# Expert 0's 0/1 columns built ahead of tile 3's normalisation, and its gather in another order

## What is computed

```python
x = layer_norm(DN_ALPHA * x + merged @ w_out[l], ln1_g[l], ln1_b[l])
# grouped_moe
probs = jax.nn.softmax(xt @ w_router + b_router, axis=-1)   # group by its two best, then top 2 inside it
gates = ...                                                  # (rows, 16), two of them not zero
for e in range(N_EXPERTS):
    h = jax.nn.silu(xt @ w_gate[e]) * (xt @ w_up[e])
    out = out + gates[:, e:e + 1] * (h @ w_down[e])
x = layer_norm(DN_ALPHA * x + moe, ln2_g[l], ln2_b[l])
```

## Time and profile before

| | |
|---|---|
| median of 3 runs | 833.96 us (833.56 to 834.3) |
| span of the profiled execution | 831.3 us |
| TensorE busy | 821.0 us, 99% of the span |
| VectorE busy | 579.2 us, 70% |
| ScalarE busy | 450.6 us, 54% |
| chain that ended last | 97% TensorE, 2% VectorE |
| mean granted TensorE clock | 0.995 |

### The profile page before, as it was taken

One profiled execution on the slowest core, in us unless ns is written; L12 is line 12 of the kernel. 1 busy time (PEld: TensorE's weight loads), 2 busy tenths in 40 slices (PEclk: granted clock), 3 DMA queues, 4 the chain that ended last, 5 costly groups with the idle time before them and its releaser, 6 DMA issues.

```text
span 831.3 us, 11149 instructions
## 1 busy us (share of the span) xinstructions
PE 821.0 (99%) x3833; PEld 682.0 (82%) x3833; DVE 579.2 (70%) x672; ACT 450.6 (54%) x456; POOL 73.3 (9%) x73
## 2 busy tenths in 40 slices
PE   9999999999999999999999999999999999999995
PEld 8888888888888888888888888888888888888873
DVE  5877434434557885432455588898899899899978
ACT  4655424433466663333233333578887887878640
POOL 1000000100000000000000000622211111100121
PEclk9999999999999999999999999999999999999999
DMA  6333324553233323234432926699999999999582
GB/s 209 93 109 90 101 84 148 200 177 101 76 101 101 101 88 114 85 94 139 151 90 77 352 102 253 203 320 418 388 393 397 395 394 390 400 377 384 227 317 106
DMA packets 112338, 173.45 MB, mean 209 GB/s; under 512 B 7402, under 2 KB 90003, under 8 KB 100534
## 3 DMA queue, kind: packets, MB, share of 16 engines
q1 hardware_dynamic: 106486, 159.80, 54.7%
q0 software_dynamic: 5824, 13.30, 4.4%
HBM read 163.49 MB, written 16.30 MB: 216 GB/s over the span
## 4 chain that ended last, share of the span: by engine, by line
PE 97%; DVE 2%; ACT 0%; issue 0%; DVEq 0%; POOL 0%; POOLq 0%
PE psA L689 8%; PE psA L691 8%; PE psA L690 8%; PE psA L876 7%; PE psA L878 7%; PE psA L877 7%; PE psB L691 6%; PE psB L690 6%; PE psB L689 6%; PE psB L903 3%; PE psB L902 3%; PE psB L901 3%; PE psD L691 2%; PE psC L691 2%; PE psD L690 2%; PE psC L689 2%
## 5 line engine op out<-in xcount | busy, mean ns | idle before, releaser
L1588 DVE TENSOR_TENSOR elo<-est,ehi 128x2048 fp32r<-128x2048 f32 x94 | 211.1, 2287 | 26.0 <-ACT ehi L1206 25.8
L1206 ACT ACTIVATE ehi<-est 128x2048 fp32r<-128x2048 f32 x94 | 177.6, 1917 | 41.5 <-DMA est<-in_w_exp_down_dram 24.9
L1378 DVE TENSOR_TENSOR wlo<-wst,whi 128x1024 fp32r<-128x1024 f32 (+1 forms) x76 | 95.0, 1251 | 86.5 <-ACT whi L1037 85.3
L1037 ACT ACTIVATE whi<-wst 128x1024 fp32r<-128x1024 f32 (+1 forms) x76 | 81.9, 1078 | 77.2 <-PE psB L691 30.7
L876 PE MATMUL psA<-ehi,xe_hi 128*128 128x512 f32 x256 | 101.4, 396 | 0.0
L878 PE MATMUL psA<-ehi,xe_lo 128*128 128x512 f32 x256 | 100.0, 390 | 0.0
L877 PE MATMUL psA<-elo,xe_hi 128*128 128x512 f32 x256 | 99.7, 390 | 0.0
L689 PE MATMUL psB<-xT_hi,whi 128*128 128x512 f32 x208 | 81.1, 390 | 0.0
L691 PE MATMUL psB<-xT_hi,wlo 128*128 128x512 f32 x208 | 81.0, 389 | 0.0
L690 PE MATMUL psB<-xT_lo,whi 128*128 128x512 f32 x208 | 81.0, 389 | 0.0
L878 PEld LDWEIGHTS psA<-ehi,xe_lo 128*128 128x128 f32 x256 | 48.1, 188 | 10.2
(11 more groups left out here) (371 smaller groups left out, 1536.3 us busy)
## 6 DMA issues: line engine op xcount, KB each, us to landing
est<-in_w_exp_gate_dram SPq DMA_DIRECT2D x32, 1024.0 KB, 12.3
est<-in_w_exp_up_dram SPq DMA_DIRECT2D x32, 1024.0 KB, 11.4
est<-in_w_exp_down_dram SPq DMA_DIRECT2D x32, 1024.0 KB, 12.5
wst<-in_w_in_dram SPq DMA_DIRECT2D x60, 512.0 KB, 3.9
wst<-in_w_branch_r_dram SPq DMA_DIRECT2D x8, 640.0 KB, 4.3
ys<-zero POOLq DMA_DIRECT2D x8, 512.0 KB, 2.9
wst<-in_w_branch_a_dram SPq DMA_DIRECT2D x8, 512.0 KB, 3.6
o_st<-in_w_out_dram SPq DMA_DIRECT2D x8, 512.0 KB, 4.4
```

The lines of the kernel that those rows point to most:

```text
L1037: A(whi[p][:, 0:K, :], wst[p][:, 0:K, :], ACT.Copy).then_inc(w_hi, 1)
L1206: A(ehi[s][:], est[s][:], ACT.Copy).then_inc(gu_hi if s < 4 else d_hi, 1)
L1378: V.tensor_tensor(wlo[p][:, 0:K, :], wst[p][:, 0:K, :], whi[p][:, 0:K, :], ALU.subtract).then_inc(w_lo, 1)
L1588: V.tensor_tensor(elo[s][:], est[s][:], ehi[s][:], ALU.subtract).then_inc(gu_lo if s < 4 else d_lo, 1)
```

## The change

Four things are changed. TensorE's two groups of unread products go from 14 to 12 and from 6 to 2. VectorE makes only expert 0's key first, and adds its positions and compares at once, so that `first_by` stands ahead of both halves of tile 3's normalisation; the keys of experts 1 to 3 are made between the halves, their additions behind. TensorE's gather for expert 0 takes tiles 0 to 2 for four blocks, waits for tile 3's half, takes tile 3 for these four, and then the same for the other four; `picks(1)` stands ahead of the last four products instead of between the halves. And VectorE's `rows_half(0)` stands right behind `listed(1)`, ahead of the row arithmetic.

```diff
             pe.wait_ge(gu_hi, 1)
-            warm(14, psC[1][:, 1, :])
+            warm(12, psC[1][:, 1, :])
...
-            warm(6, psB[0])
+            def first_rows(k, t):
+                return pe.matmul(psC[0][:, k // 4, (k % 4) * P:(k % 4 + 1) * P], x1[:, t, k * P:(k + 1) * P],
+                                 first_by[:, t, :], start=(t == 0 and k % 4 == 0),
+                                 stop=(t == TT - 1 and k % 4 == 3))
+
+            warm(2, psB[0])
             pe.wait_ge(x1_done, TT - 1)
-            pe.wait_ge(x1_half, 1)
-            for k in range(KD):
-                if k == 4:
-                    pe.wait_ge(x1_done, TT)
-                for t in range(TT):
-                    if k == 0:
-                        pe.wait_ge(first_done, t + 1)
-                    mm = pe.matmul(psC[0][:, k // 4, (k % 4) * P:(k % 4 + 1) * P], x1[:, t, k * P:(k + 1) * P],
-                                   first_by[:, t, :], start=(t == 0), stop=(t == TT - 1))
-                if k == 3:
-                    mm.then_inc(x0_t, 1)
+            for h, (done, count) in enumerate(((x1_half, 1), (x1_done, TT))):
+                for k in range(4 * h, 4 * h + 4):
+                    for t in range(TT - 1):
+                        if k == 0:
+                            pe.wait_ge(first_done, t + 1)
+                        first_rows(k, t)
+                pe.wait_ge(done, count)
+                if h == 0:
+                    pe.wait_ge(first_done, TT)
+                else:
                     pe.wait_ge(by_done, 1)
                     picks(1)
-            mm.then_inc(xe_t, 1)
+                for k in range(4 * h, 4 * h + 4):
+                    mm = first_rows(k, TT - 1)
+                mm.then_inc((x0_t, xe_t)[h], 1)
             gate_up(0, first=True, parts=range(1))
             pe.wait_ge(by_done, 2)
             picks(2)
...
             dve.wait_ge(sel_done, 1)
-            for e in range(4):
-                ins = V.tensor_scalar(keys[:, e, :], sel[:, :, e], -1000.0, 1000.0, ALU.mult, ALU.add)
-            chain.link(ins)
-
-            spread_half(TT - 1, 0, x1_half)
+            chain.link(V.tensor_scalar(keys[:, 0, :], sel[:, :, 0], -1000.0, 1000.0, ALU.mult, ALU.add))
             dve.wait_ge(pos_done, 1)
...
-            for e in range(4):
-                V.tensor_tensor(keys[:, e, :], keys[:, e, :], at_pos[:, :, e], ALU.add).then_inc(key_done, 1)
+            V.tensor_tensor(keys[:, 0, :], keys[:, 0, :], at_pos[:, :, 0], ALU.add).then_inc(key_done, 1)
             dve.wait_ge(key_done, 1)
             for t in range(TT):
                 V.tensor_scalar(first_by[:, t, :], slots[:], keys[:, 0, t:t + 1], None, ALU.is_equal
                                 ).then_inc(first_done, 1)
+            spread_half(TT - 1, 0, x1_half)
+            for e in range(1, 4):
+                ins = V.tensor_scalar(keys[:, e, :], sel[:, :, e], -1000.0, 1000.0, ALU.mult, ALU.add)
+            chain.link(ins)
             spread_half(TT - 1, 1, x1_done)
+            for e in range(1, 4):
+                V.tensor_tensor(keys[:, e, :], keys[:, e, :], at_pos[:, :, e], ALU.add).then_inc(key_done, 1)
             listed(1)
+            rows_half(0)
```

More of the change, by code:

```diff
@@ L1749, in picked, with rows_half @@
                                 None, ALU.add).then_inc(pick_done, 1)
-            for e in range(4):
-                V.tensor_tensor(keys[:, e, :], keys[:, e, :], at_pos[:, :, e], ALU.add).then_inc(key_done, 1)
+            def rows_half(q):
+                dve.wait_ge((x0_h, xe_h)[q], 1)
+                V.tensor_tensor(xe_lo[:, 4 * q:4 * q + 4], psC[0][:, q, :].rearrange("p (k c) -> p k c", c=P),
+                                xe_hi[:, 4 * q:4 * q + 4], ALU.subtract).then_inc((x0_l, xe_l)[q], 1)
+            V.tensor_tensor(keys[:, 0, :], keys[:, 0, :], at_pos[:, :, 0], ALU.add).then_inc(key_done, 1)
             dve.wait_ge(key_done, 1)
@@ L1778, in _ @@
             chain.link(V.tensor_scalar(dest[:], rowsum[:], -1.0, None, ALU.add))
[L1780 to L1785, removed]
             paid = [r16[6], r16[7]]
```

## The result

| | median | lowest to highest | executions |
|---|---|---|---|
| kernel before | 833.45 us | 833.09 to 834.30 | 8 |
| changed kernel | 835.34 us | 833.81 to 836.70 | 8 |

The ratio is 1.002, with a 95% interval of 1.001 to 1.0029: slower by 1.9 us at the median. That is small, but the whole interval lies above 1. The changed kernel scatters over 2.9 us, the kernel before over 1.2. The profiled execution of the changed kernel is one of its shorter ones, 834.16 us with a span of 832.5.

A forecast was written before the change was run, and what follows sets the result against it. TensorE's stream was taken to bound the kernel. Its gather gains 1.33 us but then waits for VectorE's list for expert 2, 0.70 later: 833.96 + 0.70 = 834.7 us, range 833.1 to 836.4.

The forecast's parts named there:

- What bounds: TensorE's stream: it waits for no DMA engine, expert turns take 17.75 us, so seam shifts reach the end one for one.
- The gather 1.33 earlier: TensorE's gather for expert 0 starts at 511.97 instead of 513.30, as its first column tile comes 1.33 us earlier.
- List 2 0.70 later: VectorE's 0/1 columns for expert 2, awaited by TensorE's picks for expert 2, end at 524.15 instead of 523.45.
- the hole before the first addition: VectorE idle for about 0.46 us, after the first key, waiting for TensorE's positions.
- The rule of free waits: Skill's rule that semaphores between chained VectorE instructions cost nothing extra; by it loss 0.45, time 834.4; forecast kept 0.70.
- The gain does not arrive: The gather's 1.33 us is lost waiting for expert 2's list; the rival that it arrives, 832.6 us, had chance 0.08.
- Nothing breaks in the queues: Queues that follow stay covered: expert 1's rows land at 524.8, wanted at 527.2, covered by 2.4 us.
- The clock: Rival: TensorE's clock halves for 3.41 us behind the wait at expert 2's picks, costing 1.7 us, 836.4; chance 0.12.
- the prediction's own sign: Forecast wrong if expert 2's picks start before 523.5, granted clock shows 0.50 between 510 and 540, or turns change length.
- the forecast case: Expert 2's picks start 0.70 us later on TensorE with no clock fall: 834.7 us, own range 834.3 to 835.3, chance 0.73.
- the clock rival: The rival described under The clock: half clock behind TensorE's new wait, 1.7 us more, chance 0.12.
- the bound of 0.2%: Smallest difference from no change a measurement can tell, 1.7 us: under 832.3 faster, over 835.6 slower.

The follow-up runs named there:

- e4: Changed kernel with VectorE's columns for expert 2 moved right behind the pick for expert 1, half 1's remainder four instructions later: 833.36 us, -0.68 against the kernel before.
- e5: e4 with VectorE's copy of the pick for expert 2 also nine instructions earlier: 832.36 us, -1.62 against the kernel before.
- e1: The changed kernel run again, unaltered, with a second trace: 835.72 us, +1.68 against the kernel before.
- e2: Changed kernel with 8 unread products in TensorE's wait ahead of the picks for expert 2: 834.59 us, +0.55 against the kernel before.

## Why the prediction was right, point by point

- **What bounds.** Right. The turns between those of the first and the last expert are 17.75 long in all three traces of the changed kernel, and a shift at the seam went through to the end. That TensorE "waits for none" of the others had less slack than it sounds: e4's 1.25 ahead was enough for expert 3's rows to come late by 0.6 to 0.9.
- **The gather 1.33 earlier.** 511.99 against 511.97 forecast.
- **List 2 0.70 later.** The picks start at 524.25 against 524.21 forecast. Counted from `sel`, which came 0.06 earlier in that execution, the list is 0.80 later. Of the missing 0.10, 0.07 is the hole before the first addition, 0.53 instead of 0.46.
- **The rule of free waits.** By the Trainium skill (VectorE: DVE Perf Modes, The DRAIN you can't avoid) the new handovers would cost nothing extra and the list would be 0.45 late. The trace has 0.80, or 0.73 without the longer hole, so for these short instructions the measurement decides against it. The rows show it directly: L1758 at 511.37 takes 0.16 and the next starts at 511.56; three keys without a wait between them take 0.30 together.
- **The gain does not arrive.** Right, and e4 and e5 show that the list was the reason: with it out of the way the picks came at 521.95.
- **Nothing breaks in the queues.** Right for expert 1's rows. The gather behind them issued at 520.18 in the profile after, as forecast. The gather for expert 2 behind it took 2.31 instead of 1.01, which the prediction had not seen: it starts inside one of VectorE's subtractions (see e4); no turn waits for it here.
- **The clock.** The mechanism and its price were right, 1.7 forecast and 1.61 measured, but **its chance of 0.12 was the term that failed**. I had put against it that wide products stand on both sides of the wait, and that the gather's stretch kept its clock with narrow ones. The traces show the stretch from 521.42 to 524.83 with TensorE busy for 1.50 of 3.41, and the clock fell behind it. By the prediction's own sign, 0.50 anywhere between 510 and 540, the forecast case failed in two of three traces. The stretch comes in two of three traces, and the 1.13 us between e1 and e2 say about as much, 0.7 of 1.61. So it belonged in the likeliest case. An estimate from the trace's 0.8, the price and this share is 0.8 + 0.7 x 1.6 = 1.9, against 1.7 to 1.9 measured; three traces are few for a share, so the agreement proves little.
- **Which executions.** The Trainium skill (TensorE: Matmul & The Clock Gate, Part 1) says that the point of change differs between runs of one kernel. The traces agree: 506.85 in one execution of the changed kernel, 524.83 and 526.16 in two others. I had cited it, and not drawn from it that a single trace with the router's slow stretch says nothing on executions without it.
- **Range and chances.** 835.34 lies in 833.1 to 836.4. As a difference the forecast did worse: 834.7 was 0.7 above the 833.96 it started from, and 1.9 was measured against a kernel before of 833.45. Well over half of the loss was not in the sum; the range holds because it had left room for the clock rival. The difference stands a little above the bound of 0.2%, which I had held to be 0.13 likely for the reason above.

## What to carry to other kernels

Where two engines arrive at the same wait within 0.1 us, an edit that speeds one and adds some tenths to the other is a loss; look for the wait behind the one that is being removed, and move the work that ends it (here list 2, then the pick) together with it. A wait of 2 us on TensorE can cost more than its length, and whether it does may vary by execution: take several traces, and don't price the clock from one. The mean granted clock of an execution tells at most whether there was such a stretch, not where. Work put ahead of a long chain on an in-order engine must have its inputs ready with slack, since whatever it waits is passed on to the end of the chain. And an engine that comes earlier can meet another's work where it didn't before, as e4's subtractions met the table writes.

## What the hardware showed that I had not expected

- In the ten traces no kernel has two half-rate stretches ahead of the end of the experts, and each stretch is 3.41 to 3.42 us long. With the wait filled or removed, executions with none appear again (mean clock 0.997 or above in 5 of 12 in e2, 5 of 11 in e5).
- TensorE counted as busy for 1.50 of the 3.41 us ahead of the fall in e1, and for all of the 3.41 us, with the router's narrow products, ahead of the fall at 506.40 in the kernel before (columns as in the earlier trace rows); the busy share of this row doesn't tell by itself where a fall follows.

```profile
502.99:506.40 3.41, 3.41 (x31) 3.29 (x29) 2.46 (x9) 1.56 (x3) 0.00 (x0) 1.00 0.99 372
```

- How long GpSimd is in an indirect DMA instruction goes by what VectorE does when it starts. In the ten traces it starts 110 gathers and table writes between 515 and 550 us. The 61 that start inside one of VectorE's 2.28 us subtractions of expert weights (`elo`) take 1.86 to 2.92, and end 0.84 to 0.92 behind that subtraction; the 49 others take 1.10 at most. Spans on GpSimd are rough, but no duration lies between the two groups. What the two engines share there no run shows.
- Executions of one kernel differ in when the filler starts (506.32, 506.75 and 507.49 in three of the changed kernel) and by up to 0.9 at the end, as much as the change moves at the seam. What sets these was not looked into.
